# Side work moved four times per weight piece instead of twice, with rests between its steps, and the delta rule's gates computed ahead of the filters

## The reference

```python
h = rms_norm(x, norm_w[l]); p = h @ w_in[l]
qa, ka, va, za, ub, zb, qkv_c, b_c, a_c, zc = _split_cols(p)
oa = sliding_window_sink_attention(qa, ka, va, sinks[l]) * silu(za)      # after rms norm and rotation
ob = conformer_conv_module(ub, ...) * silu(zb)     # depthwise filter of 31 taps, layer norm, silu, product
qkv = silu(causal_depthwise_conv(qkv_raw, conv_w)) # depthwise filter of 4 taps, 2304 channels
beta = sigmoid(b_raw)
g = -exp(a_log) * softplus(a_raw + dt_bias)        # the gates; a cumulative sum of g gives the decays
# chunks of 64 tokens, six heads of 128:
lower = where(strict, (k * beta) @ k.T * decay, 0)
u, w = solve(I + lower, [v * beta, k * beta * exp(gc)])
v_new = u - w @ S;  o = (q * exp(g)) @ S + intra @ v_new;  S = S * exp(g_last) + k'.T @ v_new
x = x + concat(oa, ob, rms_norm(oc) * silu(zc)) @ w_out[l]
```

```python
uz = rmsnorm(x) @ w_in[i]; u, z = split(uz)        # 2 x 4096 columns
uc = causal_depthwise_conv_2(u, conv_w, conv_b)    # 4 taps
r, ig = sigmoid(blocks(uc, wa) + ba), sigmoid(blocks(uc, wx) + bx)
a = exp(-8 * r * softplus(-lam)); b = sqrt(1 - a * a) * ig * uc
h[t] = a[t] * h[t - 1] + b[t]                      # a scan over the tokens
x = x + rmsnorm((h * silu(z)) @ w_out[i])
```

## Time and profile before

| what | value |
|---|---|
| median of three runs | 2882.0 us (2877.61 to 2883.11) |
| profiled execution | 2884.75 us, its span 2882.9 us |
| granted TensorE clock, mean | 0.947 |
| busy: PE, DVE, ACT | 91%, 58%, 42% of the span |
| DMA | 430.61 MB, mean 149 GB/s |
| ACT table loads | 67 |

### The profile page before, as it was taken

How to read it: one execution, slowest core, us unless ns; L and a number is a source line. 1 busy time by engine, 2 the same in 40 slices (tenths; PEclk the granted TensorE clock), 3 DMA queues, 4 the chain that set the end, 5 groups by cost and what they waited for, 6 DMA issues and landing times.

```text
span 2882.9 us, 39676 instructions
## 1 busy us (share of the span) xinstructions
PE 2618.0 (91%) x17372; PEld 2409.3 (84%) x17372; DVE 1685.1 (58%) x1866; ACT 1212.5 (42%) x1267; POOL 6.4 (0%) x14
## 2 busy tenths in 40 slices
PE   7987997889978997899999999989798998989787
PEld 7987977779978886789999999868788888888666
DVE  4787735545878546445645556555655455555654
ACT  4324234444342244344443333354545444444563
POOL 0000000000000000000000000000000000000000
PEclk9998988999989998999999999999898999999899
DMA  6432223354332223444554554535244444444433
GB/s 241 161 133 71 77 73 117 142 209 162 139 111 74 74 89 138 149 169 176 190 190 176 190 190 176 209 145 187 107 159 148 160 175 172 151 149 171 168 124 132
DMA packets 62493, 430.61 MB, mean 149 GB/s; under 512 B 6896, under 2 KB 7024, under 8 KB 12272
## 3 DMA queue, kind: packets, MB, share of 16 engines
q1 hardware_dynamic: 60496, 414.97, 39.6%
q0 software_dynamic: 1824, 13.11, 1.1%
HBM read 421.76 MB, written 6.29 MB: 148 GB/s over the span
## 4 chain that ended last, share of the span: by engine, by line
PE 70%; DVE 16%; ACT 7%; issue 5%; DMA 2%; DVEq 0%; SPq 0%; ACTq 0%
PE PS L404 69%; ACT WH L848 3%; ACT Q L834 3%; DVE WL L1336 3%; DVE Q L1305 3%; DVE Q L1301 3%; DVE Y L1305 2%; DMA W<-in_wall 2%; DVE Q L1821 1%; DVE X L1305 1%; DVE Q L1310 1%; DVE SM L1320 1%; ACT L834 0%; DVE QA L1301 0%; PE PS L654 0%
## 5 line engine op out<-in xcount | busy, mean ns | idle before, releaser
L1336 DVE TENSOR_TENSOR WL<-W,WH 128x2048 fp32r<-128x2048 f32 (+2 forms) x388 | 862.1, 2225 | 739.6 <-ACT WH L848 739.5
L848 ACT ACTIVATE WH<-W 128x2048 fp32r<-128x2048 f32 (+2 forms) x388 | 718.9, 1858 | 763.4 <-PE PS L404 730.5
L404 PE MATMUL PS<-HH,WL 128*128 128x256 f32 x3392 | 579.4, 292 | 73.9 <-DVE WL L1336 73.4
L404 PE MATMUL PS<-HL,WH 128*128 128x256 f32 x3392 | 567.5, 288 | 0.0
L404 PE MATMUL PS<-HH,WH 128*128 128x256 f32 x3392 | 566.2, 288 | 0.0
L404 PEld LDWEIGHTS PS<-HH,WL 128*128 128x128 f32 x3392 | 485.9, 198 | 84.4 <-DVE WL L1336 77.8
L404 PEld LDWEIGHTS PS<-HL,WH 128*128 128x128 f32 x3392 | 483.6, 197 | 0.0
L404 PEld LDWEIGHTS PS<-HH,WH 128*128 128x128 f32 x3392 | 482.4, 196 | 0.0
L404 PE MATMUL PS<-WL,HH 128*128 128x512 f32 (+2 forms) x768 | 229.1, 379 | 18.9 <-DVE HL L1301 12.8
L404 PE MATMUL PS<-WH,HL 128*128 128x512 f32 (+2 forms) x768 | 224.4, 373 | 0.0
L404 PE MATMUL PS<-WH,HH 128*128 128x512 f32 (+2 forms) x768 | 223.1, 371 | 0.0
(11 more groups left out here) (126 smaller groups left out, 2079.4 us busy)
## 6 DMA issues: line engine op xcount, KB each, us to landing
W<-in_wall SPq DMA_DIRECT2D x378, 1024.0 KB, 4.8
W<-in_wall SPq DMA_DIRECT2D x16, 512.0 KB, 3.4
W<-in_wall SPq DMA_DIRECT2D x8, 536.0 KB, 3.5
xsave<-X POOLq DMA_DIRECT2D x2, 2048.0 KB, 12.2
X<-xsave POOLq DMA_DIRECT2D x2, 2048.0 KB, 9.7
X<-in_x SPq DMA_DIRECT2D x4, 512.0 KB, 7.6
Q<-in_g_post POOLq DMA_DIRECT2D x2, 1024.0 KB, 4.5
Q<-in_g_ple_out POOLq DMA_DIRECT2D x2, 1024.0 KB, 6.7
```

The source lines that it names most:

```text
L404: return e.matmul(o, l, r, start=start, stop=stop, skip_group_check=True)
L848: e.activation(WH[:, s % NSPL, 0:m], W[:, c % NRAW, 0:m], ACT.Copy).then_inc(*up("hi", c))
L1336: e.tensor_tensor(WL[:, s % NSPL, 0:m], W[:, c % NRAW, 0:m], WH[:, s % NSPL, 0:m].bitcast(F32), ALU.subtract).then_inc(*up("lo", c))
```

## The change

The new kernel calls `pump()` four times per chunk on PE (after each block of a four-block chunk), on ACT and on DVE. `rest(n)` is a generator of n empty steps. In `delta_net`, `attention` and `conformer` the former single yields become rests of one to twelve moves, on all three engines alike. The taps of both filters and the conformer's taps yield after every operation instead of every two or four; the conformer gets 24 further empty moves and so takes 37 chunks instead of 31. The narrow group with the gates' inputs is moved ahead of the four wide groups (chunks 8 to 11), in the weights' order too, and the gates and decays become a generator `decays` of their own that begins behind it. In attention the third block of scores is issued before the first weights are transposed, and the keys' transposes come after 12 moves. In the output projection `add_x(0)` is done after the first group instead of together with `add_x(1)`. In the recurrent layer `conv` becomes side work for n above 0, begun where u is evicted. The pooling `windows` and the recurrent layer's `chain` keep their yields, without rests.

```diff
@@ plan
-        for c in (2048, 2560, 3584, 4096, 4608, 5120):
+        for c in (2048, 2560):
             cols("w_in", l, c, 512)
         cols("w_in", l, 5632, 268)
+        for c in (3584, 4096, 4608, 5120):
+            cols("w_in", l, c, 512)
...
+def rest(n):
+    for _ in range(n):
+        yield
@@ tensor, Group.feed
-                        if 2 * (kl + 1) == nk:
+                        for _ in range(4 * (kl + 1) // nk - 4 * kl // nk):
                             pump()
                     if half is None:
                         here["c"] += 1
-                    pump()
@@ tensor, the delta rule
-            def delta_net(l):
-                yield
+            def decays(l):
+                yield from rest(10)
                 w.wait_ge(*to("dn_v", l, "g"))
...
+            def delta_net(l):
+                yield from rest(3)
                 sq = sc(0, 3072)
                 w.wait_ge(*to("dn_a", l, "sq"))
...
-                yield
+                yield from rest(7)
                 for k in range(3):
                     b = side(("dn", l, "bt", k), ("dn_v", l, "kb", k))
@@ tensor, attention
-                yield
-                yield
-                yield
+                yield from rest(12)
                 w.wait_ge(*to("at_v", l, "kr"))
...
                 scores(0)
-                yield
+                yield from rest(3)
                 scores(1)
-                yield
-                turned(0)
+                yield from rest(4)
                 scores(2)
-                yield
+                yield from rest(2)
+                turned(0)
+                yield from rest(4)
                 turned(1)
@@ tensor, block1
-                for i in range(5):
-                    proj(l, 512 if i < 4 else 256, "cm" if i < 4 else "cm+")
+                proj(l, 256, "cm+")
+                dc = begin(decays(l), first=True)
+                for _ in range(4):
+                    proj(l, 512)
+                finish(dc)
                 dn = begin(delta_net(l), first=True)
@@ scalar and vector, tick
-                pump()
-                pump()
+                for _ in range(4):
+                    pump()
@@ scalar, taps
-                for k in range(4):
-                    if k == 3:
-                        w.wait_ge(*to("dn_v", l, "tap", i))
-                        act(CT[:, 4 * i:4 * i + n, :], CT[:, 4 * i:4 * i + n, :], ACT.Silu, "dn_a", l, "cs", i)
-                    yield
+                yield from rest(4 * n - 1)
+                w.wait_ge(*to("dn_v", l, "tap", i))
+                act(CT[:, 4 * i:4 * i + n, :], CT[:, 4 * i:4 * i + n, :], ACT.Silu, "dn_a", l, "cs", i)
@@ vector, conformer
-                        if m % 2:
-                            yield
+                        yield
+                    if k % 5 != 4 and k < 30:
+                        yield
@@ vector, block1
-                for _ in range(4):
-                    tick()
-                here["g"] += 2
-                w.wait_ge(*to("chunk", here["c"] - 1))
-                add_x(0, here["g"] - 2)
-                add_x(1, here["g"] - 1)
+                add_x(0, group(2))
+                add_x(1, group(2))
@@ vector, recurrent layer
                     for k in range(4):
+                        if n:
+                            yield
                         for m in range(4):
...
-                        ug = group(4)
+                        cv = begin(conv(n + 1, group(4)))
...
-                    if n < 7:
-                        conv(n + 1, ug)
                     tick()
```

More of the change, by code:

```diff
@@ L622, in conformer @@
             def conformer(l):
-                for _ in range(62):
-                    yield
+                yield from rest(124 + 24)
                 b = side(("cf", l, "mu"), ("cf_v", l, "mu"))
@@ L903, in delta_net @@
                 act(gs[:, 144:156], gs[:, 144:156], ACT.Exp, "dn_a", l, "e", scale=-1.0, bias=0.0)
-                act(sc(0, 3072), sc(4662, 3072), ACT.Square, "dn_a", l, "sq")
-                yield
+                yield from rest(10)
                 w.wait_ge(*to("dn_v", l, "gc"))
@@ L914, in delta_net @@
                     act(DI[:, cs], DI[:, cs], ACT.Exp, "dn_a", l, "di", k, scale=1.0, bias=0.0)
-                yield
+            def delta_net(l):
+                act(sc(0, 3072), sc(4662, 3072), ACT.Square, "dn_a", l, "sq")
+                yield from rest(3)
                 lnexp()
@@ L929, in delta_net @@
                 yield
-                yield
-                yield
-                for _ in range(10):
-                    yield
+                yield from rest(2 * 2 + 5 * 5)
                 for k in range(3):
@@ L1033, in block1 @@
                 cf = begin(conformer(l))
-                for i in range(5):
+                for i in (4, 0, 1, 2, 3):
                     g = group(4)
@@ L1446, in delta_net @@
                 tt(gs[:, 60:72], gs[:, 60:72], bt, ALU.mult)
-                yield
+            def delta_net(l, zc):
+                yield from rest(3)
                 rn = sc(0, 3072)
```

107 lines of the change are left out of this document (52 added, 55 removed).

## The result

| | median us | runs | ratio to before |
|---|---|---|---|
| before | 2882.6 | 4 (2877.6 to 2884.6) | 1 |
| changed | 2927.9 | 4 (2924.5 to 2930.1) | 1.0159 [1.0141, 1.0176] |

The forecast was 2902 us, +20; it came to +45. The direction held; attention, which should have paid for half of the loss, paid nothing.

What follows compares the result with a forecast made beforehand. PE, busy 91%, was taken to bound the kernel, with DVE and ACT mattering where PE waits. Recurrent layer +38, filters +11, attention −24, residual adds −6, pooling +1 gave +20 us: 2902 us, 8-in-10 range 2872 to 2928.

Steps and rivals of the forecast that it cites:

- What bounds the kernel: Whole kernel: PE busy 91%; its waits matter in the recurrent layer, two filter and delta stretches, two attention stretches.
- Recurrent layer: Seven gates chunks: the unrested chain and moved filter quarters lengthen one WL wait, the second goes; +38 us (+22 to +54).
- I take no difference: Recurrent layer: one longer wait in place of two changes nothing in what PE's slow clock costs; 0 us.
- rival 3: Recurrent layer: one wait instead of two saves a slow-clock stretch at six places; −12 us, 2890 us, chance 0.10.
- Filters and delta entry: Filter and delta stretches: the gates' wait returns as a wait for the square; +5.5 us per layer, +11 both.
- Attention: Both attention stretches: shorter keys' wait, no first weights' wait, later HL; −12 us per layer, −24 both (−8 to −40).
- Residual adds: Output projection: the earlier first add frees the bank in time, removing 3.08 us twice; −6 us.
- Pooling: Pooling layer: a window of the widest group behind one remainder fits the lookahead up to 0.4 us; +1 us.
- Table loads: ScalarE: loads rise from 67 to 73, priced at the trace's 1.28 us each, 8 us of ACT time.
- 1: Delta entry: DVE keeps two chunks ahead, so the square is ready when PE arrives; 2855 us, chance 0.13.
- 2: Filters and recurrent layer: idle times add up and second waits partly stay; 2923 us, chance 0.17.
- 4: Attention and recurrent layer: half way to their favourable ends, attention pays for the rest; +4 us, 2886 us, chance 0.08.

Runs made afterwards that it cites:

- b_chain: The kernel before, with the rest ahead of the third step of the recurrent layer's side chain taken out; 2901.5 us, ratio 1.0065.
- experiments 8 and 12: a_rest and c_full, in that order; 2886.5 us and 2865.0 us.
- a_taps: The changed kernel with the delta rule's taps in pairs, so a group's operations and Silu end after two chunks as before; 2923.3 us, ratio 1.0123.
- a_gates: The changed kernel with the narrow group, gates and decays back in their old place behind the wide groups; 2917.6 us, ratio 1.0104.
- a_swap: The changed kernel with ScalarE's attention exponentials one to two moves later, so the rounding WH stands ahead of them; 2888.4 us, ratio 1.0016.
- b_addx: The kernel before, with only the first half's residual add taken as soon as its group is done; 2877.7 us, ratio 0.9974.
- a_rest: The changed kernel with chain, pooling windows, filter quarters, attention, taps and gates put back, four moves and new residual add kept, rests doubled; 2886.5 us, ratio 1.0017.
- c_full: The changed kernel with exponentials behind the rounding, chain and pooling rested, filter quarters and gates in old places, taps paired; 2865.0 us, ratio 0.9922.

## Why the prediction was wrong, point by point

- *What bounds the kernel*: right. The three places named are the ones that moved.
- *Recurrent layer, +38 (+22 to +54)*: the mechanism right and the waits too (+37.2 us, one per place). Mis-sized: the clock. "I take no difference" was wrong; PE's busy time gave 9.4 us back in the changed kernel, 12.7 us in b_chain, and the term came to +27.7. It rested on a misreading: behind the 2.60 us wait I had looked at the first four products (0.74 us) and seen no loss, but the clock fell right after them. The six microseconds from there, kernel before:

```profile
2574.80:2580.80 6.00, 6.00 (x37) 6.00 (x38) 4.29 (x2) 3.71 (x4) 0.00 (x0) 0.72 0.82 302
```

  Of the six second waits only the shortest, 1.92 us, left the clock at 1.00 for the six microseconds behind it; four were followed by 0.72 to 0.74, the longest by 0.50. The Trainium skill (TensorE: Matmul & The Clock Gate, What's actually happening) has an idle engine fall to half clock and come back once it is busy. The trace agrees at these waits (0.62 behind the long one, then 1.00) and not in the narrow groups of experiments 8 and 12, where PE was busy for 39 us at 0.51 and 0.52; there the measurement decides. My −12 us for the one wait instead of two (rival 3) was close. I had given the rule a tenth and the sum nothing.
- *Filters and delta entry, +5.5 per layer*: the square's wait, the gates' wait and the moved work right; measured +8.7 and +8.2. Missed was the wait for the conformer's mean (3.47 us). The burst of sixteen taps was in the sum. By the stages a_taps puts the single taps at 4.3 and 1.0 us, a_gates the early gates at 5.4 and 4.7.
- *Attention, −12 per layer (−8 to −40)*: **the step that failed.** "The weights' wait goes, as the third scores stand between" counted the blocks on VectorE and PE and took WH as there when VectorE wants it. I had read the order of VectorE and PE and not ScalarE's against it: WH stood behind exponentials that waited for VectorE's scores, which stood behind WL. The stage from pointwise products to the norm, with the residual add, gave 1.1 us per layer (8.7 − 7.6) where 12 + 3 was forecast. With the exponentials behind WH the same stretch gave 20 (11.7 + 8.7): in a_swap the first norm's product starts at 631.74, against 643.41 before. The sum was 25 us short: attention with the adds +28, the entries +6, pooling +2, less the clock's 10 in the recurrent layer.
- *Residual adds, −6*: right (b_addx, −7). *Pooling, +1*: +2.9.
- *Table loads*: their number rose by six as the orders said (ScalarE's instructions 1267 to 1273). The Trainium skill (ScalarE: Activation LUTs, What ACT_TABLE_LOAD costs) puts a switch at 2.66 us, a drain included. In the trace the copy at 522.29 follows the load at 520.99 after its 1.28 us; ScalarE's busy time rose by 8.3 us, 6 × 1.28 being 7.7. The measurement decides.
- *Rivals*: 1 did not happen. 2's price (2923) came nearest, with another cause: not the entries and second waits, but attention. 3's mechanism is real. 4 is refuted as the kernel stood, and what it supposed of attention holds once the queue is mended.

Open: why attention's repair gave 41 us where PE's idle time fell by 27.2 (312.8 to 285.6). The other 13.2 are PE's busy time (2615.5 to 2602.3), of which the stages with attention show 10.2 (560.34 + 558.70 − 556.40 − 552.48). That fits fewer slow stretches, but no run measured the clock's share alone. Open too: what keeps the clock at half in some narrow groups, and the 10 us that a_rest lacks.

## What to carry to other kernels

When side work is spread out so that each step depends on one other engine and back, write down for every engine what stands between two pieces of the main stream's preparation, and look for a blocking wait ahead of it: put the preparation that depends on no side work (here the rounding) ahead of the work that waits. Doubling the number of moves needs every rest in a chain doubled: the recurrent chain without them cost 19 us by itself, the pooling windows 2 to 3 us. Price a merged wait by its length less the slow stretch that goes with the wait it replaces. And when differences of a few microseconds are added up, take them from the stage that the edit touches, not from ratios of whole runs.

## What the hardware showed beyond that

- Two waits close together (4.81 and 3.25 us) were followed by clocks of 0.76 and 0.50 over six microseconds each, one of 13.37 us by 0.62 and then 1.00: 5.3 us more of idle time cost less clock than the pair did.
- Twelve runs of one kernel (a_rest) range from 2882.2 to 2904.3 us, and order by their mean granted clock, 0.944 to 0.936, some 2.8 us for each 0.001; before itself had 2878.8 us at 0.948 and 2894.7 at 0.942 in one session. In the profiled executions of a_rest and c_full 17 to 18 us of such a loss are a single narrow group at half clock with PE busy all through. Kernels with the narrow group first spread over at most 7 us, those with it last over 13 to 22 (a_gates' four runs over 2). That the executions without a trace lose their time in the same place is likely and not shown. A gain in idle time has to be read with the busy time beside it.
